# Modulation by pairs of channel tiles in a two-block transformer kernel, with projections between the pairs

## Chip, cores and metric

One Trainium2 chip, one of its cores. The metric is device time of one execution in microseconds (us), the median of several runs. A granted TensorE clock of 1.00 is 2.4 GHz, 0.50 is 1.2 GHz.

## The reference, cut to what matters

Two transformer blocks are computed on 256 tokens of width 1024, in float32. The case lies in the first 140 us, the opening of the first block:

```
mx = split(silu(c) @ w_mod + b_mod, 6)          # shift, scale, gate of x; twice
mc = split(silu(c_ctx) @ w_mod + b_mod, 6)      # the same for ctx
hx = rmsnorm(x, g_norm1) * (1 + mx[1]) + mx[0]
hc = rmsnorm(ctx, g_norm1) * (1 + mc[1]) + mc[0]
px, pc = hx @ w_in, hc @ w_in                   # q k v | hq i ff fb g
f  = lb + (1 - lb) * sigmoid(ff or fb);  k = 1 - f     # forget gates of a
q  = silu(hq) * 128 ** -0.5                            # gated linear attention
```

Behind that come grouped-query attention, the two directions of the gated linear attention (chunks combined level by level), w_out, a gated MLP, and the second block.

## The kernel before, in words

All orders are written out by hand: each engine has one program, and counting semaphores tie them together. Tokens of x (256) and ctx (256) are handled side by side as 512 columns; width is cut in eight channel tiles of 128 (k = 0 to 7).

Weights stream through six slots of `raw`, 512 KB a chunk, in one list of chunks that SP issues in order (L479 to 487). Chunk n is issued once chunk n - 6 has been released: a "mod" chunk by TensorE's product with it, an "acc" chunk by VectorE's accumulation, a "w" chunk when its low half is made. A w chunk is split for precision: ScalarE copies it to `w_hi` (L620, in the first three L629), POOL subtracts to `w_lo` (L558), and TensorE takes three products per tile (`mm3`, L1457). Three slots hold split chunks; ScalarE makes chunk w once TensorE is done with w - 3. The function `hi(n)` makes all up to n - 1 at its place in ScalarE's program.

The opening goes like this. SP loads the constants, six mod chunks, then x and ctx. POOL issues 11 small loads and ten broadcasts of g_q and g_k, head by head, to `gqk` (L549 to 551). TensorE does four modulation groups g of 512 columns (L1504, 16 records of 2x512 each); VectorE copies each result row (`mod_row`, L1021), TensorE turns it to columns (`mod_cols`, L1499). VectorE scales x and ctx by rstd (L1056). When all four groups are there, VectorE sums `modc`; TensorE transposes x and ctx tile by tile (L1529); VectorE makes h (L1079, L1080), ScalarE hh (L659), and hl = h - hh is made by POOL for even k (L565) and by VectorE for odd k (L1084).

Then the projections follow, with w chunks numbered by the order of GROUPS: ff (four chunks), fb (four), hq (four), kv (two, with "diag" between them), g, q, i, g. Between w chunks the list has acc chunks by BESIDE: the gate and shift columns of w_mod, which VectorE accumulates (`acc`, L1093, L1096) in two series of eight. VectorE's order is: acc 0 to 7, decay ff (L1105 to 1108), acc 8 to 15, decay fb, hq (L1119), kd (L1122), and so on. ScalarE takes the sigmoids of ff and fb from PSUM (L665), `ga1` and hq's. `reduce_mod` sums the accumulations over the channels on TensorE. "Diag" (L1586) is the first product of the gated attention; it needs kd and the shift from acc 8 to 15. From there on levels of the gated attention alternate with the rest of the projections.

Of the kernel before, what the change touches and what calls it, by code (L numbers as in the profile page):

```python
# [46 lines left out]
C_ID, C_ONE, C_MEAN = 0, 128, 256  # L47
C_LVL = 384
# [71 lines left out]
def program(nc, a, out, orders):  # L120

    ctx = ExitStack()
    with ctx:
# [45 lines left out]
        gqk = sb("g_qk_b", [P, 640], F32, b1)  # L169
# [21 lines left out]
        r = ExitStack(); xn = sb("xn", [P, 2, D], F32, r); r.close()  # L191
        at = sb("hg_at", [P, 2, HG, T], F32, b1)
# [26 lines left out]
        r = ExitStack()  # L219
        ch = sb("cat_hi", [P, KT, T], F32R, r)  # L220
# [5 lines left out]
        kb = sb("hg_kb", [P, HG, 512], F32, r)  # L226
        r.close()
# [73 lines left out]
        GROUPS = (("ff", 1792, 512, 0, 8), ("fb", 2304, 512, 0, 8), ("hq", 768, 512, 0, 8), ("kv", 512, 256, 0, 8),  # L301
                  ("g", 2816, 512, 0, 4), ("q", 0, 512, 0, 8), ("i", 1280, 512, 0, 8), ("g", 2816, 512, 4, 8))

        BESIDE = [0, 0, 1, 2, 3, 3, 3, 3, 1]
        assert sum(BESIDE) == 2 * KT
        beside = [(k, 2048 + D * b) for b in range(2) for k in range(KT)]
        for g, c0, w, k0, k1 in GROUPS:
            kk = CHUNK // w
            for k in range(k0, k1, kk):
                add("w", w_chunk(w_in, k, kk, c0, w))  # L310
                for _ in range(BESIDE.pop(0) if BESIDE else 0):
                    at_k, at_c = beside.pop(0)
                    add("acc", w_chunk(w_mod, at_k, 1, at_c, D))
# [23 lines left out]
        W_END, w = {}, 0  # L337
        for g, n in (("ff", 4), ("fb", 4), ("hq", 4), ("kv", 2), ("g", 2), ("q", 4), ("i", 4), ("g", 2), ("out", 8)):
            w += n
            W_END[g] = w  # L340
# [12 lines left out]
        s_c = sem("cst_in")  # L353
        s_x = sem("x_in")
        s_out = sem("out_written")
# [121 lines left out]
        def _(sp):  # L477
            sp.dma_start(cst[:], a["cst"]).then_inc(s_c, 16)
            for n, (kind, parts) in enumerate(chunks):  # L479
                if n == RAW:  # L480
                    sp.dma_start(x[:], a["x"][0].rearrange("(t p) n -> p t n", p=P)).then_inc(s_x, 16)
                    sp.dma_start(cx[:], a["ctx"][0].rearrange("(t p) n -> p t n", p=P)).then_inc(s_x, 16)
                if n >= RAW:
                    released(sp, n - RAW)
                for src, p0, np_, nk, w in parts:
                    sp.dma_start(raw[p0:p0 + np_, n % RAW, 0:nk * w].rearrange("p (k n) -> p k n", k=nk),
                                 src).then_inc(s_raw[n % RAW], 16)
# [46 lines left out]
        def _(pool):  # L534
# [26 lines left out]
            lo(0, number["w"][0] % RAW)  # L561

            for k in range(0, KT, 2):
                pool.wait_ge(AC.sem, AC[f"hh {k}"])
                nc.gpsimd.tensor_tensor(hl[:, k, :], hf[:, k % 4, :], hh[:, k, :].bitcast(F32),  # L565
                                        ALU.subtract).then_inc(PL.sem, PL.tick(f"hl {k}"))
                if k < 4:
                    lo(1 + k // 2, number["w"][1 + k // 2] % RAW)
            for w, n in enumerate(number["w"]):
                if w < SPL:  # L570
                    continue
# [40 lines left out]
        def _(act):  # L612
# [42 lines left out]
            hi(3)  # L655
# [5 lines left out]
            for name, tile, b0 in (("ff", ff, 0), ("fb", fb, 4)):  # L661

                act.wait_ge(s_used, W_END[name])
                for j in range(HG):
                    nc.scalar.activation(tile[:, j, :], ps[b0 + j][:], ACT.Sigmoid).then_inc(AC.sem, AC.tick(f"sig {name} {j}"))  # L665
                hi(9 if name == "ff" else 11)
# [4 lines left out]
            hi(14)  # L671
            act.wait_ge(s_used, W_END["hq"])
            for j in range(2):
                nc.scalar.activation(flat(qf, 2 * j, 2), ps[4 + j][:], ACT.Sigmoid).then_inc(AC.sem, AC.tick(f"sig hq {j}"))
# [303 lines left out]
        def _(dve):  # L978
# [38 lines left out]
            def mod_row(g):  # L1017
                dve.wait_ge(s_mod, 4 * (g + 1))
                if g >= 2:
                    dve.wait_ge(PE.sem, PE[f"mod t {g - 2}"])  # L1020
                tick(V.tensor_copy(modrow[:, g % 2, :], ps[g][0:2, :]), f"row {g}")  # L1021

            mod_row(0)
            mod_row(1)
# [1002 lines left out]
```

## Time and profile before

| | us |
|---|---|
| median of 3 runs (995.11, 999.83, 1000.09) | 999.83 |
| span of the profiled execution (the page gives no other time of it) | 991.5 |
| TensorE busy | 891.4 (90%) |
| VectorE, ScalarE, POOL busy | 464.1, 409.5, 461.2 |
| DMA moved | 145.76 MB, mean 147 GB/s |

The page gives busy time by engine, then the span in 40 slices with TensorE's granted clock and DMA rate, then DMA queues, the chain of work that ended last, the costliest groups and the DMA issues. Rows of the time order give start and duration in us, the engine, the line, the operation, what is written from what, how many were merged, and in brackets the idle time before with what ended it. "POOL" is GpSimd, "DVE" VectorE, "PE" TensorE, "ACT" ScalarE, "SPq" the DMA queue that SyncE issues to.

### The profile page before, as it was taken

How to read it: one execution, taken by the hardware profiler on the slowest of the kernel's cores; microseconds unless marked ns; L12 is line 12 of the kernel's file. 1: busy time of each engine (PE TensorE's matmuls, PEld its weight loads, DVE VectorE, ACT ScalarE, POOL GpSimd, SP SyncE). 2: the span in 40 equal slices, each digit the busy share in tenths (PEclk: the TensorE clock that was granted, in tenths of full speed). 3: DMA queues.
4: the chain of work that ended last, by engine and by line, in shares of the span. 5: the costliest groups of instructions: out<-in, count | busy, mean ns of one | idle time of the engine just before them, and what ended most of it. 6: DMA issues, size and time to landing. Idle time of an engine off the chain costs nothing.

```text
span 991.5 us, 13660 instructions
## 1 busy us (share of the span) xinstructions
PE 891.4 (90%) x5233; PEld 740.5 (75%) x5233; DVE 464.1 (47%) x642; ACT 409.5 (41%) x627; POOL 461.2 (47%) x225
## 2 busy tenths in 40 slices
PE   5599997997988889999999699999998599999995
PEld 0157797786644669999998587877797489999994
DVE  0259856698574262333333605353325643334334
ACT  1232321215353443444435464544473534444443
POOL 4053634310003616474756398543375356564653
PEclk9799997899977989999999699999999789999998
DMA  9957841221344416656564277432344335666541
GB/s 198 270 198 237 278 122 45 84 64 52 104 121 150 128 64 181 201 170 196 172 201 137 82 217 178 141 86 85 107 137 140 106 89 189 190 189 191 178 161 42
DMA packets 89290, 145.76 MB, mean 147 GB/s; under 512 B 15260, under 2 KB 55297, under 8 KB 89249
## 3 DMA queue, kind: packets, MB, share of 16 engines
q1 hardware_dynamic: 88112, 143.23, 46.6%
q0 software_dynamic: 1104, 1.96, 1.8%
q8 instruction: 27, 0.44, 0.2%
q14 instruction: 15, 0.11, 0.0%
q10 hardware_dynamic: 32, 0.01, 0.0%
HBM read 144.13 MB, written 1.05 MB: 146 GB/s over the span
## 4 chain that ended last, share of the span: by engine, by line
PE 73%; DVE 13%; issue 5%; ACT 3%; DMA 3%; POOL 2%; SPq 0%; DVEq 0%; ACTq 0%; POOLq 0%
PE bank L1455 71%; DMA raw<-in_w_mod 3%; POOL w_lo L558 1%; ACT w_hi L620 1%; DVE hg_kb L1149 1%; DVE hg_b L1151 1%; DVE mod_acc L1096 1%; POOL z_lo L594 1%; PE bank L1659 1%; PE bank L1935 1%; DVE probs L1210 1%; DVE hg_kf L1149 1%; DVE yn L1419 1%; DVE merged_lo L1406 1%; DVE hg_f L1151 0%
## 5 line engine op out<-in xcount | busy, mean ns | idle before, releaser
L558 POOL TENSOR_TENSOR w_lo<-raw,w_hi 128x1024 fp32r<-128x1024 f32 (+2 forms) x177 | 431.6, 2451 | 488.3 <-ACT w_hi L620 446.4
L620 ACT ACTIVATE w_hi<-raw 128x1024 fp32r<-128x1024 f32 (+1 forms) x218 | 227.3, 1044 | 258.0 <-PE bank L1455 243.5
L1455 PE MATMUL bank<-z_hi,w_hi 128*128 128x256 f32 x384 | 111.8, 291 | 2.4 <-POOL z_lo L594 2.4
L1455 PE MATMUL bank<-z_lo,w_hi 128*128 128x256 f32 x384 | 110.3, 287 | 0.0
L1455 PE MATMUL bank<-z_hi,w_lo 128*128 128x256 f32 x384 | 110.1, 287 | 0.0
L1007 DVE TENSOR_TENSOR w_lo<-raw,w_hi 128x1024 fp32r<-128x1024 f32 x44 | 57.4, 1315 | 112.6 <-ACT w_hi L620 112.6
L1455 PE MATMUL bank<-n_hi,w_hi 128*128 128x256 f32 x352 | 100.8, 286 | 1.4 <-DVE w_lo L1007 0.5
L1455 PE MATMUL bank<-n_lo,w_hi 128*128 128x256 f32 x352 | 99.9, 284 | 0.0
L1455 PE MATMUL bank<-n_hi,w_lo 128*128 128x256 f32 x352 | 99.8, 284 | 0.0
L1455 PE MATMUL bank<-w_hi,mlp_h_hi 128*128 128x512 f32 x216 | 84.9, 393 | 3.0 <-DVE mlp_h_lo L1441 1.5
L1455 PE MATMUL bank<-w_lo,mlp_h_hi 128*128 128x512 f32 x216 | 84.7, 392 | 0.0
L1455 PE MATMUL bank<-w_hi,mlp_h_lo 128*128 128x512 f32 x216 | 84.5, 391 | 0.0
L1455 PEld LDWEIGHTS bank<-z_hi,w_hi 128*128 128x128 f32 x384 | 75.3, 196 | 5.2 <-issue 3.1
L1455 PEld LDWEIGHTS bank<-z_lo,w_hi 128*128 128x128 f32 x384 | 75.4, 196 | 0.6
L1455 PEld LDWEIGHTS bank<-z_hi,w_lo 128*128 128x128 f32 x384 | 75.3, 196 | 0.0
L1455 PEld LDWEIGHTS bank<-n_hi,w_hi 128*128 128x128 f32 x352 | 67.2, 191 | 3.6 <-POOL w_lo L558 1.3
L1455 PEld LDWEIGHTS bank<-n_lo,w_hi 128*128 128x128 f32 x352 | 67.3, 191 | 0.4
L1455 PEld LDWEIGHTS bank<-n_hi,w_lo 128*128 128x128 f32 x352 | 67.1, 191 | 0.0
L1455 PEld LDWEIGHTS bank<-w_hi,mlp_h_hi 128*128 128x128 f32 x216 | 40.7, 188 | 11.8 <-DVE mlp_h_lo L1441 1.9
L1439 DVE TENSOR_TENSOR mlp_h<-mlp_relu 128x512 f32<-128x512 f32 x16 | 11.1, 693 | 81.4 <-ACT mlp_relu L958 81.4
L1455 PE MATMUL bank<-raw,c_silu 128*2 128x512 f32 x64 | 32.3, 658 | 17.7 <-DMA raw<-in_w_mod 17.7
L1455 PEld LDWEIGHTS bank<-w_hi,mlp_h_lo 128*128 128x128 f32 x216 | 40.6, 188 | 8.9
(355 smaller groups left out, 1783.3 us busy)
## 6 DMA issues: line engine op xcount, KB each, us to landing
raw<-in_w_in SPq DMA_DIRECT2D x54, 512.0 KB, 4.3
raw<-in_w_down SPq DMA_DIRECT2D x54, 512.0 KB, 3.6
raw<-in_w_mod SPq DMA_DIRECT2D x48, 512.0 KB, 4.3
raw<-in_w_gu SPq DMA_DIRECT2D x44, 512.0 KB, 3.5
raw<-in_w_up SPq DMA_DIRECT2D x32, 512.0 KB, 3.6
raw<-in_w_out SPq DMA_DIRECT2D x12, 512.0 KB, 3.6
raw<-in_w_in SPq DMA_DIRECT2D x8, 336.0 KB, 3.0
raw<-in_w_out SPq DMA_DIRECT2D x8, 256.0 KB, 3.7
```

What stands on the lines that cost most here:

```text
L558: nc.gpsimd.tensor_tensor(wl[:, w % SPL, 0:size], raw[:, slot_raw, 0:size], wh[:, w % SPL, 0:size].bitcast(F32), ALU.subtract).then_inc(s_ ...
L594: nc.gpsimd.tensor_tensor(zl[:, k, :], zf[:, k % 4, :], zh[:, k, :].bitcast(F32), ALU.subtract).then_inc(PL.sem, PL.tick(f"{name}l {k}"))
L620: nc.scalar.activation(wh[:, w % SPL, 0:size], raw[:, slot_raw, 0:size], ACT.Copy).then_inc(s_hi, 1)
L1007: V.tensor_tensor(wl[:, w % SPL, :], raw[:, slot_raw, :], wh[:, w % SPL, :].bitcast(F32), ALU.subtract).then_inc(s_lod, 1)
L1096: ins = V.scalar_tensor_tensor(out=to, in0=raw[:, n % RAW, :], scalar=csil[:, k, 0:1], in1=to, op0=ALU.mult, op1=ALU.add)
L1149: ins = V.tensor_tensor(kv_[:, :, 1 - fwd, :], kv_[:, :, 1 - fwd, :], tot(fwd), ALU.mult)
L1151: done(V.tensor_tensor(fv[:, :, 0, 0:1], fv[:, :, 0, 0:1], fv[:, :, 1, 0:1], ALU.mult), f"total {n} {fwd}")
L1210: tick(V.tensor_scalar(pr[:, n % 2, :], pr[:, n % 2, :], stat[:, 160 + n:161 + n], None, ALU.mult), f"probs {n}")
L1406: tick(V.tensor_tensor(flat(mgl, k0, n), flat(mgf, k0, n), flat(mgh, k0, n).bitcast(F32), ALU.subtract), f"merged lo {b}")
L1419: ins = V.scalar_tensor_tensor(out=yn[:, t, 512 * j:512 * j + 512], in0=ps[bank + 2 * t + j][:], scalar=stat[:, 216 + t:217 + t], in1=gpos ...
L1439: V.tensor_tensor(h2[:, g % 3, :], rr[:, g % 3, :], rr[:, g % 3, :], ALU.mult).then_inc(s_h2, 1)
L1455: return nc.tensor.matmul(out_, l, r_, start=start, stop=stop, skip_group_check=True)
```

## The change

The first third of w_mod (shift and scale) are taken in four groups that each hold the shift and scale of one pair of channel tiles (2g, 2g + 1), as two pieces of 256 columns in rows of 1 KB. The first pair is done ahead; every further one stands between the two halves of a forget-gate chunk, followed by a query chunk of the same channel tiles. So ff and hq are projected side by side, in banks 0 to 3 and 4 and 5, and fb comes after both, in banks 0 to 3. VectorE does the modulation by pairs (`modulation(g)`, `h_pair(g)`), with all eight hl itself.

x and ctx are loaded first, behind the part of the constants that is used at once; the rest of the constants follows at chunk 12. They are transposed as they are, copied by VectorE from PSUM to `x_T_a`, `x_T_b`, and multiplied there by rstd, which TensorE spreads over the partitions by one product of ones with four diagonals. The ten broadcasts of g_q and g_k become two of 64 columns each, issued by POOL ahead of w chunk 14 and broadcast over the heads when read. VectorE does acc 0 and 1 ahead of the last pair, 2 to 7 behind it, then the angles, hq, decay ff, acc 8 to 15, decay fb, kd. The diff, cut:

```diff
-        for g in range(4):
+        mod_pairs = w_mod[:, 0:2 * D].rearrange("(k p) (s n) -> p k s n", p=P, s=2)
+
+        def add_mod(g):
             for k in range(0, KT, 2):
-                add("mod", w_chunk(w_mod, k, 2, 512 * g, 512))
-        BESIDE = [0, 0, 1, 2, 3, 3, 3, 3, 1]
+                add("mod", *[(mod_pairs[:, k + j, :, 256 * g:256 * g + 256], 0, P, 2, 256) for j in range(2)])
+        BESIDE = [0, 0, 0, 1, 1, 2, 2, 2, 2, 2, 2, 2]
+        add_mod(0)
+        for j in range(4):
+            add_in(2 * j, 2, FF_AT, 512)
+            if j < 3:
+                add_mod(j + 1)
+            add_in(2 * j, 2, HQ_AT, 512)
+        for k in range(0, KT, 2):
+            add_in(k, 2, FB_AT, 512)
...
-            sp.dma_start(cst[:], a["cst"]).then_inc(s_c, 16)
+            sp.dma_start(cst[:, 0:C_FIRST], a["cst"][:, 0:C_FIRST]).then_inc(s_c, 16)
+            sp.dma_start(x[:], a["x"][0].rearrange("(t p) n -> p t n", p=P)).then_inc(s_x, 16)
+            sp.dma_start(cx[:], a["ctx"][0].rearrange("(t p) n -> p t n", p=P)).then_inc(s_cx, 16)
...
-            for h in range(10):
-                v = a["g_q"] if h < 8 else a["g_k"]
-                pool.dma_start(gqk[:, HD * h:HD * h + HD], v[0:1, :].broadcast_to([P, HD])).then_inc(s_bc, 16)
...
+                if w == W_END["kv"]:
+                    for j, v in enumerate((a["g_q"], a["g_k"])):
+                        pool.dma_start(gqk[:, j, :], v[0:1, :].broadcast_to([P, HD])).then_inc(s_bc, 16)
...
             for k in range(KT):
+                if k % 2 == 0:
+                    hi(k + 1)
                 act.wait_ge(DV.sem, DV[f"h {k}"])
                 nc.scalar.activation(hh[:, k, :], hf[:, k % 4, :], ACT.Copy).then_inc(AC.sem, AC.tick(f"hh {k}"))
-            hi(5)
+            hi(8)
+            gate_sigmoids("ff", ff)
+            hi(10)
+            act.wait_ge(s_used, W_END["hq"])
+            for j in range(2):
+                nc.scalar.activation(flat(qf, 2 * j, 2), ps[4 + j][:], ACT.Sigmoid).then_inc(AC.sem, AC.tick(f"sig hq {j}"))
+            hi(13)
+            gate_sigmoids("fb", fb)
+            hi(14)
...
+            def h_pair(g):
+
+                for k in (2 * g, 2 * g + 1):
+                    own(f"xn {k}")
+                    if k >= 4:
+                        own(f"hl {k - 4}")
+                    V.tensor_scalar(hf[:, k % 4, 0:T], xT(k)[:, 0:T], modc[:, 8 + k, 0:1], modc[:, k, 0:1], ALU.mult, ALU.add)
+                    tick(V.tensor_scalar(hf[:, k % 4, T:2 * T], xT(k)[:, T:2 * T], modc[:, 8 + k, 1:2], modc[:, k, 1:2],
+                                         ALU.mult, ALU.add), f"h {k}")
+                for k in (2 * g, 2 * g + 1):
+                    dve.wait_ge(AC.sem, AC[f"hh {k}"])
+                    tick(V.tensor_tensor(hl[:, k, :], hf[:, k % 4, :], hh[:, k, :].bitcast(F32), ALU.subtract), f"hl {k}")
...
+            acc(0, 0)
+            acc(0, 1)
+            modulation(3)
+            h_pair(3)
+            for k in range(2, KT):
+                acc(0, k)
...
+            decay("ff", ff, kf, 0)
+            for k in range(KT):
+                acc(1, k)
+            decay("fb", fb, kb, 1)
...
+            for k in range(5):
+                x_by_channel(k, k)
+            pe.wait_ge(DV.sem, DV["csil"])
+            mod_rows(0, 0, 2)
...
+            for k in range(5, KT):
+                pe.wait_ge(DV.sem, DV[f"xT {k - 5}"])
+                x_by_channel(k, k - 5)
+            mod_rows(0, 2, 6)
+            pe.wait_ge(DV.sem, DV["x diag"])
+            mm(ps[5][:], ones, dg4[:].rearrange("p t k -> p (t k)"), True).then_inc(PE.sem, PE.tick("x rstd"))
+            mod_rows(0, 6, 8)
...
+            for j in range(4):
+                s = split(w_at[0])
+                for kk in range(2):
+                    k = 2 * j + kk
+                    pe.wait_ge(DV.sem, DV[f"hl {k}"])
+                    for h, (o, _) in enumerate(to_f):
+                        c = 512 * kk + P * h
+                        ins = mm3(o, wh[:, s, c:c + P], wl[:, s, c:c + P], hh[:, k, :], hl[:, k, :], k == 0, k == KT - 1)
+                    if kk == 0 and j < 3:
+                        mod_rows(j + 1)
+                ins.then_inc(s_used, 1)
+                w_at[0] += 1
+                if j < 3:
+                    mod_cols(j + 1)
+                if j == 0:
+                    pe.wait_ge(DV.sem, DV["xn 7"])
+                s = split(w_at[0])
+                by_channel(s, 2, 2 * j, hh, hl, T, to_hq).then_inc(s_used, 1)
+                w_at[0] += 1
+            pe.wait_ge(AC.sem, AC["sig ff 3"])
+            project("fb", to_f, True)
+            reduce_mod(0)
```

## Rows read from the trace of the kernel before

**Rows 1.** Busy time by windows: stretch, length, busy of each engine, clock, DMA share, GB/s.

```profile
12.00:30.00 18.00, 7.55 (x17) 1.10 (x15) 0.68 (x1) 0.00 (x0) 0.55 (x2) 0.93 0.98 105
30.00:42.00 12.00, 5.98 (x9) 0.83 (x9) 0.00 (x0) 6.38 (x11) 0.00 (x0) 0.54 1.00 379
...
43.60:47.20 3.60, 3.60 (x10) 0.75 (x9) 3.08 (x18) 0.21 (x1) 0.00 (x0) 1.00 0.70 237
```

**Rows 2.** DMA issues: queue, count, KB each, median us from issue to landing.

```profile
x<-in_x SPq DMA_DIRECT2D x1, 1024.0 KB, 27.4
...
g_qk_b<-in_g_q POOLq DMA_DIRECT2D x8, 32.0 KB, 11.8
```

**Rows 3.** The chain that ended last, 0 to 145 us: start, us, what.

```profile
10.67 25.30 DMA raw<-in_w_mod
...
42.79 6.96 PE bank L1455 x16
...
58.22 0.60 PE bank L1529 x4
...
69.27 16.75 PE bank L1455 x72
...
114.50 11.84 PE bank L1455 x101
```

**Rows 4.** TensorE in order of time: first projection, first reduce, diag.

```profile
62.58 0.47 PE L1455 MATMUL bank<-h_hi,w_hi 128*128 128x512 f32 x1
...
111.06 1.13 PE L1455 MATMUL bank<-mod_acc,cst 128*128 128x512 f32 x2 [2.15 <-ACT hg_b L665]
...
133.54 1.95 PE L1455 MATMUL bank<-hg_q,hg_kd 128*128 128x128 f32 x16
```

**Rows 5.** VectorE groups, 0 to 130 us: busy, mean ns, idle before.

```profile
L1079 DVE TENSOR_SCALAR h_f<-bank,mod_cols 128x256 f32<-128x256 f32 x8 | 4.3, 535 | 2.9 <-PE bank L1529 2.9
...
L1084 DVE TENSOR_TENSOR h_lo<-h_f,h_hi 128x512 fp32r<-128x512 f32 x4 | 3.4, 851 | 0.7 <-ACT h_hi L659 0.7
...
L1021 DVE COPY mod_rows<-bank 2x512 f32<-2x512 f32 x4 | 2.7, 677 | 40.3 <-PE bank L1455 40.3
```

**Rows 6.** VectorE in order of time, 73 to 132 us.

```profile
73.67 10.74 DVE L1096 SCALAR_TENSOR_TENSOR mod_acc<-raw,c_silu,mod_acc 128x1024 f32<-128x1024 f32 x5
84.69 2.67 DVE L1096 SCALAR_TENSOR_TENSOR mod_acc<-raw,c_silu,mod_acc 128x1024 f32<-128x1024 f32 x2 [0.28 <-DMA raw<-in_w_mod]
88.14 4.00 DVE L1105 TENSOR_SCALAR hg_f<-hg_f,lb_cols 128x512 f32<-128x512 f32 x4 [0.77 <-ACT hg_f L665]
...
95.50 1.23 DVE L1108 TENSOR_SCALAR hg_f<-hg_f 128x2048 f32<-128x2048 f32 x1
...
127.45 1.29 DVE L1119 SCALAR_TENSOR_TENSOR hg_q<-bank,hg_qf 128x512 f32<-128x512 f32 x2 [7.87 <-ACT hg_qf L674]
128.78 3.06 DVE L1122 TENSOR_TENSOR hg_kd<-hg_kf,hg_kb 128x1024 f32<-128x1024 f32 x1
...
131.84 1.21 DVE L1126 TENSOR_TENSOR hg_qf<-hg_q,hg_f 128x1024 f32<-128x1024 f32 x1
```

**Rows 7.** ff's sigmoids; one weight chunk's issue, copy and low half, in time.

```profile
86.03 2.07 ACT L665 ACTIVATE hg_f<-bank 128x512 f32<-128x512 f32 x4 [8.73 <-PE bank L1455]
...
100.33 0.38 SPq L486 DMA_DIRECT2D raw<-in_w_in  x1
...
105.64 1.06 ACT L620 ACTIVATE w_hi<-raw 128x1024 fp32r<-128x1024 f32 x1 [6.07 <-DMA raw<-in_w_in]
...
106.78 3.27 POOL L558 TENSOR_TENSOR w_lo<-raw,w_hi 128x1024 fp32r<-128x1024 f32 x1 [4.21 <-ACT w_hi L620]
```

**Rows 8.** TensorE in order of time, behind an idle gap.

```profile
182.07 0.44 PE L1455 MATMUL bank<-hg_qf,hg_kf 128*128 128x64 f32 x2 [2.20 <-DVE hg_b L1151]
```

**Rows 9.** Busy time by windows behind that gap, columns as rows 1.

```profile
184.00:186.00 2.00, 2.00 (x13) 2.00 (x13) 1.16 (x2) 0.00 (x0) 0.38 (x1) 0.58 0.53 129
```

More of the change, by code:

```diff
@@ L309, in program @@
             for k in range(k0, k1, kk):
[L310 to L313, printed above, removed]
+                add_in(k, kk, c0, w)
         for b in (2, 3):
@@ L353, in program @@
         s_c = sem("cst_in")
+        s_cl = sem("cst_late_in")
         s_x = sem("x_in")
+        s_cx = sem("ctx_in")
         s_out = sem("out_written")
@@ L1015, in _, with x_from_psum, x_normed @@
                                  stat[:, 0:16].rearrange("p (v k) -> p v k", v=2), ALU.mult), "csil")
[L1017 to L1024, printed above, removed]
-            V.tensor_copy(idb[:], ident)
-            V.tensor_copy(msk[:], cst[:, C_CAUS:C_CAUS + P])
+            xT = lambda k: (xTa if k < 4 else xTb)[:, k % 4, :]
+            def x_from_psum(k, bank):
+                dve.wait_ge(PE.sem, PE[f"xT {k}"])
+                tick(V.tensor_copy(xT(k), ps[bank][:]), f"xT {k}")
+            def x_normed(k):
+                own(f"xT {k}")
+                tick(V.tensor_tensor(xT(k), xT(k), ps[5][:], ALU.mult), f"xn {k}")
+            for k in range(6):
+                x_from_psum(k, k % 5)
             dve.wait_ge(PE.sem, PE["rows"])
@@ new lines, in _, with modulation @@
+            tick(ins, "x diag")
+            x_from_psum(6, 1)
+            x_from_psum(7, 2)
+            dve.wait_ge(PE.sem, PE["x rstd"])
+            x_normed(0)
+            x_normed(1)
+            def modulation(g):
+                dve.wait_ge(s_mod, 4 * (g + 1))
+                tick(V.tensor_copy(modrow[:, g % 2, :], ps[6][0:2, :]), f"row {g}")
+                dve.wait_ge(PE.sem, PE[f"mod t {g}"])
+                pair = modc[:].rearrange("p (s k) v -> p s k v", s=2)[:, :, 2 * g:2 * g + 2, :]
+                bias = cols[:, R_BMOD:R_BMOD + 16].rearrange("p (s k) -> p s k", s=2)[:, :, 2 * g:2 * g + 2]
+                done(V.tensor_tensor(pair, ps[7][:, 160 + 8 * g:168 + 8 * g].rearrange("p (s k v) -> p s k v", s=2, k=2),
+                                     bias.unsqueeze(3).broadcast_to([P, 2, 2, 2]), ALU.add), f"modc {g}")
+                done(V.scalar_tensor_tensor(out=modc[:, 8 + 2 * g:10 + 2 * g, :], in0=modc[:, 8 + 2 * g:10 + 2 * g, :], scalar=1.0,
+                                            in1=cols[:, R_G1 + 2 * g:R_G1 + 2 * g + 2].unsqueeze(2).broadcast_to([P, 2, 2]),
+                                            op0=ALU.add, op1=ALU.mult), f"modc scale {g}")
@@ L1058, in _ @@
+            modulation(0)
+            h_pair(0)
+            for k in range(2, KT):
+                x_normed(k)
             dve.wait_ge(AC.sem, AC["lb exp"])
@@ L1108, in decay @@
                 done(V.tensor_scalar(f[:], f[:], 1.0, None, ALU.min), f"{name} min")
-            for k in range(KT):
-                acc(0, k)
-            decay("ff", ff, kf, 0)
-            for k in range(KT):
-                acc(1, k)
-            decay("fb", fb, kb, 1)
+            acc(0, 0)
+            acc(0, 1)
+            modulation(3)
+            h_pair(3)
+            for k in range(2, KT):
+                acc(0, k)
+            dve.wait_ge(s_pos, 16)
+            done(V.tensor_copy(stat[:, 200:202], pos[:]), "pos")
+            A0, A1, A2, A3 = (ang[:, j, :] for j in range(4))
+            pf = lambda v: v.rearrange("p (t f) -> p t f", t=2)
+            done(V.tensor_tensor(pf(A0), stat[:, 200:202].unsqueeze(2).broadcast_to([P, 2, 24]),
+                                 cst[:, C_INV:C_INV + 24].unsqueeze(1).broadcast_to([P, 2, 24]), ALU.mult), "ang")
+            done(V.tensor_scalar(A1, A0, 1.0 / (2 * math.pi), ROUND, ALU.mult, ALU.add), "turns r")
+            done(V.tensor_scalar(A1, A1, ROUND, None, ALU.subtract), "turns")
+            for j, part in enumerate(TWO_PI):
+                done(V.tensor_scalar(A2, A1, part, None, ALU.mult), f"turn {j}")
+                done(V.tensor_tensor(A0, A0, A2, ALU.subtract), f"r {j}")
+            done(V.tensor_scalar(A0, A0, PI, -PI, ALU.min, ALU.max), "r")
+            done(V.tensor_scalar(A3, A0, -1.0, None, ALU.mult), "-r")
+            done(V.tensor_tensor(A3, A0, A3, ALU.max), "|r|")
+            tick(V.tensor_scalar(A1, A3, -1.0, math.pi / 2, ALU.mult, ALU.add), "angles")
+            V.tensor_copy(idb[:], ident)
+            dve.wait_ge(s_cl, 16)
+            V.tensor_copy(msk[:], cst[:, C_CAUS:C_CAUS + P])
             dve.wait_ge(AC.sem, AC["sig hq 1"])
```

192 lines of the change are left out of this document (77 added, 115 removed).

## Prediction

> **What bounds the kernel now.** I read the page's timeline first, then the busy time by windows, then the chain of waits, then each engine in order of time between 0 and 134 us. Behind 134 us nothing of the order changes except a few small operations, so the case is decided by one instant: the start of "diag", the first product that needs kd, at 133.54 us [rows 4]. What follows it hangs on the same engines in the same order before and after, and I carry the shift of that instant to the end one to one.
>
> Until 42 us DMA sets the pace. Between 12 and 30 us the DMA engines are 0.98 busy and move 105 GB/s; between 30 and 42 us they are 1.00 busy and move 379 GB/s [rows 1]. What differs is the ten g_q and g_k broadcasts, 128 rows of 256 bytes each, of which the eight of g_q land a median 11.8 us after issue; x, issued at 4.76 us, takes 27.4 us [rows 2]. The chain stands on one modulation chunk for 25.30 us [rows 3], and TensorE idles into the half clock (mean 0.54 in 30 to 42 us, 1.2 of 2.4 GHz being 0.5). From 36 to 62 us the chain is TensorE's: each of four modulation groups is 16 records in 6.96 us [rows 3]. Projections begin at 62.58 us [rows 4] and run nearly without a gap to diag. VectorE keeps up: it ends kd at about 131.8 us, 1.7 us ahead [rows 4, 6].
>
> **Part 1, the front.** Removed: the ten broadcasts' place ahead of everything (two stay, issued in a stretch with spare DMA time), four row scalings on VectorE, the wait for the whole modulation before the first h. At 379 GB/s (rows 1), from about 3 us on, the small constants, x and ctx (2.24 MB) are in by 9.6 us; the four chunks of the first pair, 0.52 MB each, follow by 15.4 us. TensorE then has, behind ctx: 20 transposes (0.15 us each by 0.60 for four, the double at the half clock; 3.7 taken), 12 more (1.8), two small ones (0.4), the modulation group of pair 0 (6.96), and the rstd product (0.9): 9.6 + 3.7 + 1.8 + 0.4 + 6.96 + 0.9 = 23.4 us for the last modulation product. VectorE's eight copies out of PSUM, its eight products with rstd and the diagonal lie beside this, some before and some after. Then the row copy 0.7, four small transposes 0.4, two small sums 0.45, h of two tiles in four halves 1.8, hl 0.8 (ScalarE's hh lies beside the second tile) [rows 3, 5]: 23.4 + 0.7 + 0.4 + 0.45 + 1.8 + 0.8 = 27.6 us for the first projection, 35 us earlier than now. A half tile of h is priced at 0.45 to 0.54 (from PSUM, rows 5); from SBUF it can be less, and I keep 0.45.
>
> The 1 KB rows of the modulation chunks (2 KB before) have no row here at full DMA load. Both ends: 379 GB/s, or the 105 GB/s of 12 to 30 us, which came with 256-byte rows; nearest are the weight loads, so I take 379. The Trainium skill (DMA: Bandwidth & Descriptors, Bandwidth) asks for DMAs of 1 MiB or more and lists 138 GB/s for 64 KB against 341 for 1 MB; the modulation now comes in 256 KB pieces. By a rate midway the first pair would land some 3 us later, in front of TensorE work that is late anyway.
>
> **Part 2, the pairs.** Per pair TensorE does 12 projection products (12 x 0.233 = 2.8 us, from 16.75 us for 72), a modulation group (6.96), 12 more (2.8), transposes (0.35), and 24 query products (24 x 0.117 = 2.8, from 11.84 us for 101; 2.9 with the change-over) [rows 3]: 15.8 us. Three pairs are 47.4, plus 0.2 to 0.3 of waiting for hl each: the third query chunk ends at 75.3. The last h pair on VectorE (72.2 + 0.45 + 1.8 + 1.5) ends at 75.9. Against now (h done at about 72.8, ahead of rows 6) this is 3 us later for VectorE, though TensorE has by then three quarters of ff and hq behind it. DMA has slack here: six chunks and an accumulation chunk in 15.8 us need 3.7 MB, 9.7 us at 379 GB/s. The late constants (0.7 MB) cost SP one issue and DMA 1.9 us, hidden in the same slack. POOL loses four h_lo, VectorE gains them, within the 0.85 us rows [rows 5].
>
> **Part 3, ff's end to diag: where the gain goes.** Work left for TensorE from 75.3: ff 5.6, hq 2.9, fb 22.4, reduce 3.5 (111.06 to the next product at 114.5), half of kv 5.6, a second reduce estimated at half of that, 1.9: 42, diag at 117.3 if nothing waited [rows 3, 4]. Two things wait.
> First, fb's first chunk. ScalarE makes it only after ff's four sigmoids, and its DMA slot hangs on acc 2 and 3, which VectorE starts at 75.9. Issued about 81, landed 85, ScalarE 1.06 and POOL 2.7 to 3.3 give 89 [rows 7]; TensorE ran dry at 84. Five us of stall.
> Second, fb's last chunk. In the new order its DMA issue stands behind that of an accumulation chunk whose slot is freed by acc 9, and acc 8 and 9 come on VectorE after the angles, hq and the whole ff decay. VectorE from 75.9: six accumulations at 1.33 alone and 2.15 beside POOL's w_lo [rows 6], 8 to 13, taken 10; the angles, moved here, 3.5 (43.6 to 47.2, rows 1) and two copies, with one collision 5; hq's sigmoid is out by 91 (ScalarE makes two weight chunks first), hq 1.3; ff decay 8.6 (88.14 to 96.7); acc 8 and 9 2.1. That is 103. The chunk needs 5.3 us from issue to ScalarE's start, 1.06, then 3.3 on POOL [rows 7]: 112 to 113, taken 111.5. TensorE, with fb 0 to 2, is through by 106 to 109. Fb ends at 117.
> Then four sigmoids 2.1 [rows 7], fb decay 8.6, kd 1.2 to 3.1: 129 to 131. TensorE has reduce, half of kv and the second reduce, 11.1, and is at diag at 128.1 to 129. Diag starts at 129.5, 4.0 us earlier than 133.54. The ends of the unknown terms (accumulations 8 or 13, decays 6.5 or 8.6 each, kd 1.2 or 3.1) move this by -7 to +5 us.
>
> Small: g_q and g_k as broadcasts over heads turn two products into three, 0.3 us at about 218 us in VectorE's chain; left out. POOL's two DMA issues (0.54 us each) stand ahead of the g weights, 3 to 6 us before TensorE wants them; if that cover were gone they would cost 1.1.
>
> Kd of 128x1024 took 3.06 us beside a w_lo, the same shape alone 1.21 [rows 6]. The Trainium skill (SBUF — State Buffer, Who interferes with whom) has VectorE and GpSimd share a port pair as an exclusive lock, also for a VectorE operation with two SBUF inputs. The trace agrees; by it, each of the four moved hl, and each accumulation, can cost up to a w_lo (2.4 us) more.
>
> **The sum.** From the first projection to diag it is now 133.54 - 62.58 = 70.96 us. Added to that stretch: three modulation groups 20.9, their transposes and waits for hl 1.7, the stalls ahead of fb 0 and fb 3 (5.0 + 5.7), kd's tail 1.4. Gone from it: transposes and the two short waits of now, 3.4. That is 102.3, from 27.6: 129.9 by this count, 129.5 by the walk; 133.54 - 129.5 = 4.0 us. The page's span 991.5 becomes 987.5. The page gives the span alone; the median of three runs, 999.83, is 8.3 above it, the lowest, 995.11, 3.6 above. I take 4 off the median: 995.8.
>
> **The rivals.**
> (a) Faster by more: the two gates don't bite, since accumulations run at 1.33, and the copies on DMA land early. Speaking for it: two accumulations in 2.67 us at 84.69 [rows 6]. Then TensorE's work alone bounds diag, 117.3 to 124, a gain of 9 to 16: 984 to 991, middle 987. Against it: the order on VectorE is fixed, and decay stands ahead of acc 8 whatever the pace. Chance 0.25.
> (b) Slower: TensorE's clock. An idle gap of 2.20 us ending at 182.07 was followed by a clock of 0.58 in 184 to 186, the half clock for most of it [rows 8, 9]; the long idle before 36 us by 0.54 [rows 1]. The new waits lie ahead of fb 0 (5 us), fb 3 (2 to 7) and diag (1 to 3). The mechanism decides once the wait ahead of fb 3 exceeds about 3 us: then fb 3 runs at half clock (+5.6), and after kd's wait the rest of kv and the first level (+5). 4 - 10.6 is 6.6 us slower: 1006.4. The Trainium skill (TensorE: Matmul & The Clock Gate, What's actually happening) says "the default state is throttled, and activity releases the throttle"; these rows agree. Chance 0.15.
> (c) The front doesn't gain what it should: ctx lands late or the 1 KB rows are slow, so that pair 0 is 4 us later and everything behind with it. Equal: 1000. This is also the case in which the change doesn't do what it says. Chance 0.15.
> The forecast, 990 to 999, has 0.45.
>
> **How the numbers follow.** A difference within 0.5%, 5 us, is about what runs of this kernel can't tell from none. Faster: all of (a), and 0.17 of the forecast (gains of over 5): 0.42. Slower: (b), and a tail of (c): 0.16. Within: 0.42. The range leaves out half of (b) and the far end of (a): 986 to 1004. Cases of both signs hold chance; the forecast's own range is 990 to 999.
>
> **What would show it.** In the trace after: ctx landed by 10 us and no stretch at 105 GB/s (part 1); the first projection product at 27 to 29 us; 15.8 us from pair to pair; the third query chunk ending near 75; ScalarE's w_hi of fb's last chunk idle before it "<-DMA", starting at 107 to 109; kd at 126 to 129; diag at 129.5. What would make the prediction wrong: VectorE's accumulations at other durations than part 3 takes, or a shift at diag that isn't the shift at the end.

## The result, and the profile after

The change makes the kernel slower: 1007.06 us median (1005.72 to 1009.97, 4 runs) against 999.54 us (995.11 to 1000.09, 4 runs), a ratio of 1.0079 with an interval of 1.0053 to 1.0106. Forecast were 995.8 us and a range of 986 to 1004. The profiled execution took 1007.23 us with a span of 1005.4; that of before has a span of 991.5 and is one of its quick ones. So the profiles lie 13.9 us apart and the medians 7.5. I use the profiles to place the loss, and ratios from runs for its size.

The window of after that answers to the first of rows 1, columns as there:

```profile
12.00:30.00 18.00, 14.43 (x51) 6.59 (x50) 12.40 (x30) 5.93 (x8) 3.82 (x2) 0.90 0.79 253
```

The chain of waits of after, from ctx to the second pair (start, us, what):

```profile
1.67 7.47 DMA ctx_rows<-in_ctx
...
9.28 4.14 PE bank L1574 x20
...
27.42 15.68 PE bank L1512 x40
43.10 0.33 PE bank L1556 x4
43.44 15.79 PE bank L1512 x64
59.23 0.34 PE bank L1556 x4
```

The front did what part 1 said: ctx is in at 9.1 us, the first projection stands at 27.42 against 62.58 [rows 4], and the stretch at 105 GB/s [rows 1] is one at 253, with TensorE busy in 14.4 of its 18 us. 35 us are won here. The same chain from the last h on shows who spends them:

```profile
80.99 1.29 DVE mod_acc L1129
...
88.75 7.52 DMA raw<-in_w_in
96.30 0.03 ACT w_hi L641
...
97.26 1.07 ACT hg_qf L696 x2
...
98.97 0.69 DVE hg_q L1170
99.69 1.93 DVE hg_f L1138 x4
101.64 3.32 DVE hg_kf L1140
...
107.11 1.29 DVE mod_acc L1129
...
108.79 6.94 DMA raw<-in_w_in
115.75 1.07 ACT w_hi L641
...
116.89 2.35 POOL w_lo L586
...
119.28 7.15 PE bank L1512 x24
...
128.56 4.02 DVE hg_b L1138 x4
132.60 4.25 DVE hg_kb L1140
136.87 3.42 DVE hg_b L1141
140.31 1.23 DVE hg_kd L1177
...
141.68 8.36 PE bank L1512 x52
```

Before, the chain in the same place is TensorE's but for two sigmoid waits (16.75 and 11.84 us in single pieces, rows 3). Now it goes from VectorE to a DMA, back to VectorE, to another DMA, and through the whole decay of fb. Diag starts at 141.68, 8.1 us later than before [rows 4]. Three gaps on TensorE belong to it (TensorE in order of time, idle before in brackets):

```profile
94.86 0.76 PE L1512 MATMUL bank<-h_hi,w_hi 128*128 128x512 f32 x1 [4.03 <-POOL w_lo L586]
...
119.28 0.79 PE L1512 MATMUL bank<-h_hi,w_hi 128*128 128x512 f32 x1 [5.91 <-POOL w_lo L586]
...
141.68 3.76 PE L1512 MATMUL bank<-hg_q,hg_kd 128*128 128x128 f32 x16 [4.38 <-DVE mod_cols L1180]
```

And the windows of after:

```profile
100.00:104.00 4.00, 4.00 (x19) 3.25 (x18) 3.97 (x5) 1.06 (x1) 2.59 (x1) 1.00 0.02 4
...
108.00:112.00 4.00, 4.00 (x19) 3.25 (x18) 3.68 (x4) 0.00 (x0) 0.00 (x0) 1.00 0.81 257
112.00:116.00 4.00, 1.37 (x6) 0.76 (x5) 1.85 (x2) 0.25 (x1) 0.00 (x0) 0.92 0.93 291
116.00:120.00 4.00, 0.72 (x2) 0.62 (x3) 2.99 (x1) 1.01 (x2) 2.34 (x1) 0.50 1.06 378
...
140.00:144.00 4.00, 2.32 (x11) 2.34 (x12) 3.93 (x6) 0.00 (x0) 0.00 (x0) 0.50 0.44 131
```

From 100 to 108 us the DMA engines are idle, 0.02 busy over these 8 us. SP issues in order, and the next chunk of its list takes the slot of accumulation chunk 8, which VectorE releases at 107.0, once the decay of ff is over; the loads then come in one burst. Behind the second and the third gap the granted clock is 0.50, the lower level of 1.2 GHz.

### The profile page after: what moved, and what is told of

The parts are those of the page before. It is cut to its first block, busy times and chain, and to the rows that moved or that the text cites. A ratio compares the mean times of both kernels' runs of the same rounds, so it can differ in the third digit from the quotient of the medians.

```text
span 1005.4 us, 13727 instructions
## 1 busy us (share of the span) xinstructions
PE 903.9 (90%) x5235; PEld 751.7 (75%) x5235; DVE 475.8 (47%) x669; ACT 409.4 (41%) x627; POOL 449.7 (45%) x213
## 4 chain that ended last, share of the span: by engine, by line
PE 69%; DVE 16%; issue 6%; ACT 4%; POOL 2%; DMA 2%; SPq 0%; DVEq 0%; POOLq 0%; ACTq 0%
PE bank L1512 67%; DVE mod_acc L1129 2%; DMA raw<-in_w_in 1%; POOL w_lo L586 1%; POOL z_lo L615 1%; ACT w_hi L641 1%; DVE hg_kb L1204 1%; DMA ctx_rows<-in_ctx 1%; DVE hg_b L1206 1%; PE bank L1732 1%; PE bank L2010 1%; DVE probs L1267 1%; DVE hg_kf L1204 1%; DVE yn L1476 1%; PE bank L1574 1%
## 5 line engine op out<-in xcount | busy, mean ns | idle before, releaser
L1512 PE MATMUL bank<-h_hi,w_hi 128*128 128x256 f32 (+1 forms) x128 | 47.5, 371 | 14.5 <-POOL w_lo L586 9.9
L1512 PEld LDWEIGHTS bank<-w_hi,mlp_h_hi 128*128 128x128 f32 x216 | 40.7, 188 | 11.7 <-DVE mlp_h_lo L1498 1.9
```

The lines of the kernel that those rows point to most:

```text
L1512: return nc.tensor.matmul(out_, l, r_, start=start, stop=stop, skip_group_check=True)
```

## The experiments

"kd ends" is where VectorE finishes the sum that diag waits for, the last step of the disputed stretch. "Rest" is the span less that instant. Times are medians; the ratio is to the kernel before, run beside it.

| kernel | first projection | kd ends | span | rest | time | ratio |
|---|---|---|---|---|---|---|
| before | 62.6 | 131.8 | 991.5 | 859.7 | 999.5 | |
| after | 27.4 | 141.5 | 1005.4 | 863.9 | 1007.1 | 1.0079 [1.0053, 1.0106] |
| a_beside | 27.8 | 134.4 | 995.5 | 861.1 | 998.9 | 0.9994 [0.9967, 1.0021] |
| a_accfirst | 28.6 | 135.0 | 999.7 | 864.7 | 998.2 | 0.9982 [0.9954, 1.0011] |
| a_angles | 28.9 | 143.2 | 1003.8 | 860.6 | 1004.9 | 1.0064 [1.0035, 1.0093] |
| a_fill | 28.0 | 139.4 | 997.8 | 858.4 | 1002.2 | 1.0027 [1.0004, 1.0051] |
| a_early | 29.0 | 130.5 | 993.6 | 863.1 | 992.1 | 0.9946 [0.9917, 0.9974] |
| a_hqback | 31.8 | 133.4 | 995.2 | 861.8 | 996.0 | 0.996 [0.9933, 0.9987] |
| a_hqback_early | 32.4 | 131.5 | 999.7 | 868.2 | 998.6 | 0.998 [0.995, 1.001] |
| a_wide | 38.9 | 152.7 | 1017.5 | 864.8 | 1019.9 | 1.0196 [1.0142, 1.025] |
| b_small | 44.7 | 115.7 | 979.3 | 863.6 | 981.9 | 0.9814 [0.9761, 0.9866] |
| b_small_x | 47.1 | 118.2 | 982.0 | 863.8 | 985.1 | 0.9865 [0.9831, 0.9899] |
| b_small_fill | 44.8 | 115.9 | 983.8 | 867.9 | 986.8 | 0.9873 [0.983, 0.9915] |

The rest is 858 to 868 us in all thirteen while kd's end moves by 37 us: that instant decides in the main, as the forecast had it. Of the two rests of 868, one (a_hqback_early) has diag 2 us behind kd, where it waits for TensorE, and the other (b_small_fill) has a filler behind kd. The other eleven lie from 858 to 865; the least is that of a_fill, where the clock is held up.

**Which part of the change wins, which loses: b_small and a_wide.** b_small is the kernel before with the broadcasts alone taken over from the change:

```diff
-            for h in range(10):
-                v = a["g_q"] if h < 8 else a["g_k"]
-                pool.dma_start(gqk[:, HD * h:HD * h + HD], v[0:1, :].broadcast_to([P, HD])).then_inc(s_bc, 16)
...
+                if w == W_END["kv"]:
+                    for j, v in enumerate((a["g_q"], a["g_k"])):
+                        pool.dma_start(gqk[:, j, :], v[0:1, :].broadcast_to([P, HD])).then_inc(s_bc, 16)
```

> The kernel before with one part of the change alone: g_q and g_k as two small broadcasts issued ahead of weight chunk 14, instead of ten ahead of everything. Theory C: the broadcasts held the load queue from 12 to 30 us and nothing else did. Then the modulation runs on TensorE's own 28 us, the first projection starts near 43 us instead of 62.6, and diag comes 15 to 20 us earlier, since the order behind is as it was: 980 to 985. Rival D: behind the front the loads can't follow (they move 280 GB/s in 86 to 112 us already), and the gain shrinks to under 8 us, above 992.

a_wide is the changed kernel with this part undone (ten broadcasts ahead of everything):

> The changed kernel with the ten broadcasts of before put back ahead of everything and read as before. Theory C: x and ctx are issued first and land nearly in time, but the first pair's four modulation chunks share the queue with the broadcasts at about 105 GB/s, the first projection comes 10 to 15 us later than at 27.4, and the kernel is 8 to 15 us slower than the changed one, 1015 to 1022. Rival: with x ahead in the queue the broadcasts cost little (under 3 us).

Both came out as expected. b_small gains 18 us, and is the fastest kernel of the study; a_wide loses 20. So all the rest of the change, the new order, costs 20 us with the broadcasts in place (a_wide against before), and 25 without them (after against b_small, 1007.1 - 981.9). It holds more than the pairs: x and ctx come first, and rstd is applied behind the transposes; no run takes these away one by one. The windows of b_small and then of a_wide, to be laid beside rows 1:

```profile
12.00:30.00 18.00, 17.22 (x45) 3.58 (x44) 5.86 (x26) 6.60 (x12) 0.00 (x0) 1.00 1.04 394
```

```profile
12.00:30.00 18.00, 9.64 (x37) 3.62 (x35) 6.60 (x17) 1.64 (x3) 0.52 (x1) 0.89 0.96 94
```

With two broadcasts instead of ten, 394 GB/s in place of 105, and TensorE busy in 17.2 of these 18 us. This is what I had not seen: the pairs were to fill a TensorE that stood idle in the front, and taking the broadcasts out of the way is enough to fill it. The chain of b_small between 60 and 150 us:

```profile
74.06 17.02 PE bank L1456 x72
...
93.22 35.31 PE bank L1456 x276
```

It is TensorE's, diag within it, as before, 16 us earlier.

**What gates fb's last chunk: a_beside and a_accfirst.** The first loads the last eight accumulation chunks behind fb's weights, the second takes those accumulations ahead of hq and of the decay of ff on VectorE.

```diff
-        BESIDE = [0, 0, 0, 1, 1, 2, 2, 2, 2, 2, 2, 2]
+        BESIDE = [0, 0, 0, 1, 1, 2, 2, 2, 0, 0, 0, 8]
```

> The changed kernel with accumulation chunks 8 to 15 moved behind fb's last weight chunk in the load list. Theory A (the slot ring): fb's last chunk stood behind accumulation chunks whose slots wait for VectorE's acc 9, and that wait cost most. Then fb's last product group starts near 112 us instead of 119.3, diag near 131 instead of 141.7, and the kernel is some 10 us faster than the changed one, about 996. Theory B (the low clock and port collisions in 86 to 142 us cost it, the slot wait only hides them): diag moves by under 3 us, about 1004.

```diff
+            for k in range(KT):
+                acc(1, k)
             dve.wait_ge(AC.sem, AC["sig hq 1"])
...
             decay("ff", ff, kf, 0)
-            for k in range(KT):
-                acc(1, k)
             decay("fb", fb, kb, 1)
```

> The changed kernel with VectorE's order turned: acc 8 to 15 ahead of hq and of ff's decay. Theory A: the same gate is opened from the other side, fb's last chunk is issued near 100 us instead of 108.4, its products start near 112, diag near 130, the kernel about 10 us faster, 996. Theory B: VectorE's work ahead of kd is a plain sum and its order moves nothing, diag within 3 us of 141.7, 1004 to 1007.

Each takes 8 to 9 us off, and in each the gap ahead of fb's last chunk is gone while those ahead of fb and of diag stay. Diag stands at 134.56 in a_beside and 135.18 in a_accfirst, 3.6 and 5.2 us later than I had written. TensorE in order of time, a_beside:

```profile
134.56 3.77 PE L1512 MATMUL bank<-hg_q,hg_kd 128*128 128x128 f32 x16 [4.87 <-DVE mod_cols L1180]
```

So the gate is real and worth 8 us. Without it the changed kernel equals the one before; it doesn't beat it.

**Angles: a_angles.** The angles ahead of the second pair, where VectorE is idle.

> The changed kernel with the angles (16 small VectorE operations, 5.8 us at 91 to 97) moved ahead of pair 1, where VectorE is idle. If they stand on the chain, as the prediction had it, diag moves by 4 to 6 us and the kernel takes about 1002. If hq's sigmoid on ScalarE ends last there (it waits for a weight chunk to land and comes out at 98.3, 1.3 us after VectorE is free), at most 1 us is gained: 1006 to 1007.

This takes 2 us off, between the two expectations. In its trace VectorE then waits 6.57 us for the query's sigmoid, which starts at 96.98 (97.26 in after): it stands on ScalarE behind a weight copy that waits for its DMA. So the angles weren't what held VectorE up there. This trace has diag at 143.3, later than after, and doesn't show where the 2 us come from.

**The clock: a_fill.** Fourteen products more on TensorE, whose results nobody uses:

```diff
+            def fill(bank, n):
+                for _ in range(n):
+                    mm(ps[bank][:], ident, x[:, 0, 0:512], True)
             pe.wait_ge(AC.sem, AC["sig ff 3"])
-            project("fb", to_f, True)
+            fill(6, 4)
+            project("fb", to_f, True, after=[lambda: None, lambda: None, lambda: fill(6, 6), lambda: None])
...
                 reduce_mod(1)
+                fill(7, 4)
                 diag()
```

> The changed kernel with 14 idle-time products on TensorE (512 columns, results unused): 4 ahead of fb's first chunk, 6 ahead of its last, 4 ahead of diag, each set shorter than the wait it stands in. Theory G: the three waits (4.0, 5.9, 4.4 us) let the clock fall to 0.5, which costs 1.5 us at fb's last chunk (7.15 us for 24 products instead of 5.6) and about 3 behind diag. Then the granted clock stays 1.00 from 86 to 155 us, the first level ends 3 to 5 us earlier than at 155.0, and the kernel takes 1002 to 1004. Rival: the clock falls anyway or its loss lies in later waits; then the time is that of the changed kernel, 1007, or longer by the products' own time.

5 us less, as expected. Windows of after, then of a_fill:

```profile
112.00:134.00 22.00, 16.09 (x86) 13.15 (x86) 11.84 (x9) 7.15 (x10) 9.79 (x6) 0.84 0.72 243
134.00:160.00 26.00, 21.62 (x170) 21.55 (x169) 16.84 (x15) 4.15 (x5) 7.35 (x4) 0.87 0.32 81
```

```profile
112.00:134.00 22.00, 21.65 (x114) 16.23 (x113) 13.56 (x9) 7.36 (x11) 11.54 (x6) 1.00 0.79 264
134.00:160.00 26.00, 21.98 (x165) 19.54 (x164) 18.70 (x16) 5.01 (x6) 10.68 (x4) 1.00 0.28 70
```

The clock stays at 1.00 from 112 to 160, and work that nobody wants makes the kernel faster. Some 5 of the 25 us between after and b_small are the clock; the remaining 20 are not.

**Accumulations among the pairs: a_early.** Eight accumulations ahead of the last pair, with their chunks moved up in the load list, the angles ahead of the second pair, four more accumulations and the decay of ff ahead of hq, and fb's first chunk copied ahead of ff's sigmoids. The edit of the list:

```diff
-        BESIDE = [0, 0, 0, 1, 1, 2, 2, 2, 2, 2, 2, 2]
+        BESIDE = [0, 2, 2, 2, 2, 2, 2, 0, 0, 2, 2, 0]
```

> The changed kernel with VectorE's work brought into its idle stretches between the pairs: eight accumulations ahead of the last h pair instead of two, their chunks moved up in the load list; angles ahead of pair 1; four more accumulations, then ff's decay, ahead of hq; fb's first chunk copied ahead of ff's sigmoids. Theory E: what the order by pairs costs is that VectorE's chain behind the last h (accumulations, two decays, kd: 61 us) starts at 81 us, with TensorE's covering work already spent. Then diag comes near 118 to 122 us instead of 141.7 and the kernel takes 982 to 988, no better than the kernel of before with small broadcasts (982), since TensorE's work then bounds both. Rival F: the pairs themselves cost it (crowded load slots, 1 KB rows): with more chunks among the pairs these grow longer than 15.8 us, and diag stays above 130.

The best of the pair order, 15 us off, but 4 short of theory E, with diag at 130.6 instead of 118 to 122. Both signs of rival F are there too: diag stays above 130, and the pairs have grown from 16.13 us to 18.05 and 17.27 (transposes at 43.58, 61.63 and 78.90). Part of that is VectorE, which accumulates until 60.2 with 4.74 us of waiting for a chunk in it before it copies the row; how much is F's doing no run tells. Its chain from fb to diag:

```profile
92.77 22.56 PE bank L1517 x96
...
117.52 7.09 DVE hg_b L1160 x4
...
124.63 1.24 DVE hg_kb L1162
...
125.89 3.35 DVE hg_b L1163
...
129.26 1.23 DVE hg_kd L1182
```

TensorE computes fb without a gap of any size, and then diag waits for fb's sigmoids, decay and sum: 15.2 us from fb's end at 115.3 to 130.5. TensorE has only the two reduces and half of kv for that, and idles 4.38 us. In before and in b_small the query stands in this place (33.65 and 35.31 us of unbroken chain behind fb), and the same decay costs nothing. This asked for a test.

**The query behind fb again: a_hqback and a_hqback_early.** Pairs with the forget gate alone, the next pair's modulation ahead of this pair's gate, then fb, query, kv; VectorE takes the query behind both decays. Both lists also carry accumulation chunks earlier than after does, and the second kernel takes six accumulations between the pairs and the angles ahead of the second pair:

```diff
             for j in range(4):
+                if j < 3:
+                    mod_rows(j + 1)
...
-                s = split(w_at[0])
-                by_channel(s, 2, 2 * j, hh, hl, T, to_hq).then_inc(s_used, 1)
...
-            project("fb", to_f, True)
+            pe.wait_ge(DV.sem, DV["xn 7"])
+            project("fb", [(ps[4 + j][:], True) for j in range(4)], True)
+            pe.wait_ge(AC.sem, AC["sig fb 3"])
             reduce_mod(0)
-            pe.wait_ge(AC.sem, AC["sig fb 3"])
+            project("hq", to_hq, True, T)
```

> The changed kernel with the first query projection taken out of the pairs and put behind the backward gate, as in the kernel before: order forward gate, backward gate, query, keys and values. In the pairs the modulation of the next pair now stands ahead of the forward gate's products, so that it covers the steps that make h; the backward gate goes to banks 4 to 7 and waits for no sigmoid. VectorE takes the query behind both decays. In its trace the changed kernel has about 9 us of TensorE's work (keys and values) behind the backward gate's last product before its diagonal must start, and VectorE needs 14 us there (sigmoids 2, decay 11.7, sum 1.2): idle 4.4. Theory C (cover: what the change costs is that the query's 12 us of products have been spent ahead of the backward gate): the idle time ahead of the diagonal is gone or under 1.5 us, none of 3 us or more stands ahead of the backward gate or in it, diagonal at 122 to 128, time 984 to 991. Rival L (VectorE's length: its 60 us of accumulations, decays and sums behind the last h decide, wherever the query stands): the last h stands at about 65, the diagonal at 65 + 60 + 4 of angles = 129 or later, time 992 or more. Rival P (the pairs themselves cost): the forward gate ends later than 75 and the time is above 995.

> The same with the angles ahead of the second pair and six accumulations taken between the pairs (two behind pair 1, four behind pair 2), so that VectorE has about 10 us + 4 us less behind the last h. Theory C: TensorE's own work is the bound, nothing more to be had than by the query's place: within 3 us of the run above, 982 to 988, and not below the kernel before with the two small broadcasts alone (981.9), since that one has TensorE busy in 95.4 of the 100 us from 12 to 112 already. Rival L: it gains 8 us or more on the run above.

The theory of cover falls as the whole cause: 996.0, not 984 to 991, and diag at 133.53 with 3.13 us idle ahead of it. Rival L had written 129 or later and 992 or more, and that held. So did both signs of rival P (forward gate later than 75, time above 995): the gate ends at 78.4 and the time is 996.0. The last h is ready at 72.2, not at 65. The chain of waits of a_hqback has two chunks inside the pairs:

```profile
49.34 6.03 DMA raw<-in_w_in
...
60.71 3.84 DMA raw<-in_w_mod
```

The first holds up ScalarE, which makes this chunk's high half before the next h's, and the second VectorE, which accumulates before it copies the modulation row. TensorE then waits 3.25 us for that row.

Behind that, VectorE runs from its last h to kd with only two short waits for a chunk (VectorE in order of time, a_hqback):

```profile
72.16 10.18 DVE L1129 SCALAR_TENSOR_TENSOR mod_acc<-raw,c_silu,mod_acc 128x1024 f32<-128x1024 f32 x6
...
114.24 8.14 DVE L1138 TENSOR_SCALAR hg_b<-hg_b,lb_cols 128x512 f32<-128x512 f32 x4
122.41 3.30 DVE L1140 TENSOR_SCALAR hg_kb<-hg_b 128x2048 f32<-128x2048 f32 x1
125.74 4.13 DVE L1141 TENSOR_SCALAR hg_b<-hg_b 128x2048 f32<-128x2048 f32 x1
129.90 1.29 DVE L1174 SCALAR_TENSOR_TENSOR hg_q<-bank,hg_qf 128x512 f32<-128x512 f32 x2
131.23 2.16 DVE L1177 TENSOR_TENSOR hg_kd<-hg_kf,hg_kb 128x1024 f32<-128x1024 f32 x1
```

72.2 to 133.4 is 61 us. Up to diag VectorE is busy for 93.2 us here, 80.7 in after, 71.3 in before and 71.6 in b_small. The 12.5 us between a_hqback and after aren't more work. Both have 116 operations up to kd, which would take 63 us if each took the shortest time that its form shows in these runs; the traces have 34 us on top in a_hqback and 22 in after, and in both all but 2 us of it in operations that overlap one of POOL's subtractions. The four scalings of hg_b are an example: 8.14 us beside three w_lo here, 4.01 in after. In before and b_small it is 90 operations, 52 us, and 20 and 21 on top. So of the 60 us that rival L took as VectorE's length, a large part (25 of a_hqback's 61) lies in such overlaps and moves with the order.

Rival L fell in its turn with the second run: taking six accumulations out of this stretch should have given 8 us, and gave none (998.6). There VectorE waits 9.37 us for the query's sigmoid and diag starts at 133.52 with 0.26 us idle; TensorE is late instead, held up inside the pairs:

```profile
39.18 0.58 PE L1561 MATMUL bank<-cst,mod_rows 2*128 2x2 f32 x4 [5.16 <-DVE mod_rows L1082]
...
71.91 0.50 PE L1561 MATMUL bank<-cst,mod_rows 2*128 2x2 f32 x4 [3.64 <-DVE mod_rows L1082]
```

VectorE is now inside TensorE's loop four times (row copy, sums, h, hl). In this kernel the angles stand ahead of the row copy of the first of these gaps and four accumulations ahead of that of the second; what isn't given between the pairs lies behind the last. Chunks that come late add to it here too: VectorE waits 5.99 us for one to accumulate, and ScalarE 16.86 us for one to copy, with 5.71 us of VectorE's waiting for the h behind it. In b_small the last h ends at 55 us and VectorE has 60 us for what follows, under TensorE's projections; in after it ends at 81.

**Could b_small be mended further: b_small_x, b_small_fill.** The first loads x and ctx behind two modulation chunks; the second adds 14 products (results unused) ahead of the second level, where b_small has 5.58 us idle and a clock of 0.50 behind it.

> The kernel before with small late broadcasts and x and ctx issued behind the second modulation chunk. With the broadcasts gone, x and ctx land by 19 us and are wanted near 29, so loading them earlier gains nothing: 981 to 984. If anything it is slower by up to 3 us, since modulation chunks 2 to 5 land 5 us later while TensorE waits for them.

> The kernel before with the two small late broadcasts, and 14 more products (results unused) on TensorE ahead of the second level's scores, where its trace shows 5.6 us idle (134.3 to 139.8) and then a granted clock of 0.50 from 140 to 150. Theory G (the idle time costs the clock): the clock stays at 1.00 there, some 10 us of work at half speed take 5 us less, time 976 to 980. Rival: the products delay the level by as much as they save, or the clock falls anyway at the next gap: 981 to 983.

Neither gains. x earlier costs 3 us. In b_small_fill the clock holds at 1.00 from 134 to 154 (0.66 in b_small), yet it is 5 us slower: I sized the filler wrongly. In the trace the 14 products fill 12.18 us, 0.87 each, not 5.6, and start the second level at 146.34 rather than 139.84; and the level behind it, which starts on VectorE's word, then has the gap of 5.21 us instead (160.87). A filler of the right size wasn't tried.

## Why the prediction was wrong

The step that failed is part 3, the walk from ff's end to diag. It put diag at 129.5, 4.0 us earlier than before, and the trace has it at 141.7, 8.1 us later. It had VectorE begin 5 us too early (3.6 of them from part 2), put fb's last chunk, fb's last products and the decay of fb too short (2.4, 1.6 and 2.8 us below), and put TensorE's low clock at nothing outside rival (b).

**Part 1 held.** First projection 27.42 for 27.6, last modulation product 23.5 for 23.4. The Trainium skill (DMA: Bandwidth & Descriptors, Bandwidth) would have the 256 KB pieces slower. The page of after has them landing in 5.1 us (median) against 3.9 for the 512 KB chunks of the same matrix; it stayed hidden, since no product of the first pair waits for a chunk. One term is off without harm: 2.24 MB at 379 GB/s from 3 us on are in by 8.9, not 9.6, and ctx landed at 9.1.

**Part 2 was 3.6 us short.** Two causes. TensorE had been idle for 2.70 us when the first projection began, and its twelve products came 0.43 us apart, not 0.233; the modulation group behind them took 7.31. That is 2.9 us by the transposes of pair 1 (43.1 for 40.2). The window behind the gap:

```profile
28.00:32.00 4.00, 4.00 (x11) 3.12 (x10) 4.00 (x7) 1.50 (x2) 3.48 (x2) 0.50 0.01 5
```

The clock stood among my rivals, with this very kind of gap in rows 8, and I did not look for gaps of that kind in my own walk. And the period is 16.13 us for 15.8, 0.3 a pair. (The walk also added the 0.2 to 0.3 us of waiting for hl once and not three times; in the trace the next products wait for no hl until the last pair.)

**Part 3 failed.** Walk and trace, each row's own share being the difference of the delays:

| step | walk | trace | own share |
|---|---|---|---|
| last hl ends | 75.9 | 81.0 | +5.1 |
| accumulations 8 and 9 done | 103 | 108.4 | +0.3 |
| fb's last products start | 111.5 | 119.3 | +2.4 |
| fb ends | 117 | 126.4 | +1.6 |
| diag | 129.5 | 141.7 | +2.8 |

*Last hl:* the 3.6 of part 2 and 2.2 for a collision, less some 0.6 by which h and hl were quicker than priced (VectorE and POOL of after, in order of time):

```profile
75.93 2.34 DVE L1088 SCALAR_TENSOR_TENSOR mod_cols<-mod_cols,cols 128x4 f32<-128x4 f32 x1
```

```profile
75.86 2.39 POOL L586 TENSOR_TENSOR w_lo<-raw,w_hi 128x1024 fp32r<-128x1024 f32 x1 [2.92 <-ACT w_hi L641]
```

A sum over 128x4, 0.17 us otherwise, takes as long as POOL's subtraction beside it. The Trainium skill's exclusive lock (SBUF — State Buffer, Who interferes with whom) gives just that, and the trace agrees; I had priced it for hl and the accumulations, not for a small operation in TensorE's loop.

*Accumulations 8 and 9:* the sum was right by luck. Hq came at 98.4, not 91, since ScalarE's query sigmoid stood behind a w_hi that waited for its chunk until 96.30; the decay of ff took 6.5 instead of 8.6. *Fb's last chunk:* 1.2 of the 2.4 us are a slip: 103 + 5.3 + 1.06 + 3.3 is 112.7, and I took 111.5. The rest is the landing, 6.94 us, and 7.3 from issue to ScalarE's start against 5.3 forecast, partly made good by POOL (2.35 for 3.3). The loads held back since 100 us come down together in these 7 us, at 257 and 291 GB/s (windows 108 to 116); that this is what makes the landing long is argued, not tested. *Fb ends:* 24 products in 7.15 us for 5.5, at half clock behind 5.91 idle: rival (b)'s mechanism. *Diag:* the decay of fb took 11.7 us, not 8.6. Beside it POOL made three w_lo and issued the two broadcasts, whose place I had priced at TensorE only. That POOL made it longer is read from the overlap; the same three operations took 8.5 us in before.

Behind diag the first level ends at 154.99 for 144.71 before: 2.1 us more, half clock behind the 4.38 us gap. Some three more come in the next levels (the shift is 10.0 us at 225.57 of before and 13.3 at 254.57), where 18 products took 5.71 us instead of 3.09; at the end it is 13.9. By these two profiles the one-to-one carry thus held within about 6 us (8.1 at diag, 13.9 at the end).

Rival (b) gave 1006.4, and the time is 1007.1. That the two numbers agree is luck. It was right that the clock would cost; a_fill puts that at 5 us, half of the 10.6 it claimed. The rest lies in the other rows of the table: VectorE's late start, the last chunk and the decay of fb. And the frame of the forecast was wrong: I booked 35 us of earlier start as 4 us of gain and asked only where the stalls are. b_small shows that 18 of these 35 us come without the pairs, with the old order behind them intact. Priced apart, the two halves of the change are a gain of 18 us and a loss of 25.

What stays open is how the 20 us beyond the clock divide between VectorE (its operations and POOL's part in them), the query's place, and the loads inside the pairs. a_early takes work off VectorE behind the last h and meets the missing cover (diag at 130.6); a_hqback puts the query back and meets VectorE (133.5); a_hqback_early does both and loses it inside the pairs (133.5). No run removes one of the three and leaves the others as they were. How much of the 7.5 or 13.9 us falls behind 200 us isn't settled by single profiles either.

## What to carry to other kernels

When a change has a cheap half and a deep half, price them apart. Here the cheap one (eight small broadcasts fewer) removed the very idle time that the deep one was to fill. An earlier start of one engine is worth only what the slowest list behind it lets through: sum each engine's work from the last shared input to the instant that decides, before and after, and look at what runs beside it: the same 116 operations of VectorE took 81 us in after and 93 in a_hqback. And ask what covers a decay before moving it: in before and b_small the query stood over the decay of fb, in after and a_early little does, and TensorE idles 4.38 us. No run isolates how much of the loss that is.

## What the runs showed of the hardware

Ten broadcasts of 128 rows of 256 bytes held the loads of the other queue at 94 to 105 GB/s from 12 to 30 us (a_wide, before); with two of them later it is 394 (b_small). An operation of 0.17 us on VectorE lasts 2.34 us if POOL's subtraction of 128x1024 began just before (after, at 75.93). Idle times of TensorE of 2.70, 5.91 and 4.38 us in after were each followed by a clock of 0.50, one of 0.86 us in a_hqback was not (sixteen modulation products behind it took 7.03 us, the full pace). The length alone doesn't tell: 2.15 us of idle time were followed by a mean clock of 0.58 in b_small (93 to 97 us) and of 1.00 in before (111 to 115 us). Unused products in the gaps ahead of fb, of its last chunk and of diag gave back 5 us (a_fill).
